# Attention head steps taken two projection units ahead, the output projection by weight rows, table parts made between head pairs, one split moved in the sparse heads

## What is computed

```python
def dilated_attention_mixer(h, positions, w_qkv, w_o):      # 3 groups, 8 heads of 128
    qkv = (h @ w_qkv).reshape(b_, s_, 3, g_ * hh, dh)
    q = partial_rotary(qkv[:, :, 0], positions)...           # k the same; v = qkv[:, :, 2]
    for g, (window, dilation) in enumerate(DILATED_PATTERNS):
        o_g, lse_g = dilated_window_attention(q[:, :, g], k[:, :, g], v[:, :, g], window, dilation)
    weights = jax.nn.softmax(jnp.stack(lses, axis=0), axis=0)
    o = jnp.sum(weights[..., None] * jnp.stack(outs, axis=0), axis=0)
    return o.reshape(b_, s_, hh * dh).astype(h.dtype) @ w_o
```

## Time and profile before

| what | value |
|---|---|
| runs of the kernel, us | 1976.30, 1976.33, 1984.96; median 1976.33 |
| profiled execution, its own time | 1978.76 us |
| its span, first to last instruction | 1977.0 us |
| PE busy | 1890.6 us (96%) |
| DVE / ACT / POOL busy | 66% / 47% / 31% |
| granted TensorE clock, mean | 0.976 |
| DMA | 336 MB, 170 GB/s |

### The profile page before, as it was taken

How to read it: one execution, slowest core, us unless ns; L and a number is a source line. 1 busy time by engine, 2 the same in 40 slices (tenths; PEclk the granted TensorE clock), 3 DMA queues, 4 the chain that set the end, 5 groups by cost and what they waited for, 6 DMA issues and landing times.

```text
span 1977.0 us, 31728 instructions
## 1 busy us (share of the span) xinstructions
PE 1890.6 (96%) x13371; PEld 1725.6 (87%) x13371; DVE 1300.1 (66%) x1506; ACT 935.9 (47%) x1223; POOL 620.1 (31%) x752
## 2 busy tenths in 40 slices
PE   8999999899998999999999899999999997899999
PEld 7989999899997899989997789998799985678998
DVE  6877776665564777866667666667466656547665
ACT  4354454443443544554443254445544445555443
POOL 6968871543343877800001610000000000321000
PEclk9999999999999999999999799999999988899999
DMA  6556664444432656566554335654355531005552
GB/s 236 183 181 228 209 235 160 145 163 160 159 129 85 211 212 228 201 238 255 190 192 165 113 132 213 220 214 158 100 186 201 204 131 64 22 1 195 189 192 107
DMA packets 54826, 336.35 MB, mean 170 GB/s; under 512 B 7915, under 2 KB 13084, under 8 KB 17820
## 3 DMA queue, kind: packets, MB, share of 16 engines
q1 hardware_dynamic: 45648, 297.51, 41.9%
q10 hardware_dynamic: 5068, 22.13, 3.0%
q0 software_dynamic: 3968, 14.68, 2.3%
HBM read 318.54 MB, written 15.75 MB: 169 GB/s over the span
## 4 chain that ended last, share of the span: by engine, by line
PE 79%; DVE 10%; ACT 6%; issue 3%; POOL 1%; ACTq 0%; DVEq 0%; POOLq 0%
PE psum L478 22%; PE psum L431 12%; PE psum L433 12%; PE psum L432 12%; PE psum L480 11%; DVE w_lo L1819 4%; ACT w_hi L1077 3%; DVE both L1826 1%; ACT both L1077 1%; PE psum L1028 1%; PE psum L876 1%; PE psum L997 1%; PE psum L1014 1%; DVE h L1832 1%; ACT sq L1101 1%
## 5 line engine op out<-in xcount | busy, mean ns | idle before, releaser
L1819 DVE TENSOR_TENSOR w_lo<-raw,w_hi 128x2048 fp32r<-128x2048 f32 x277 | 652.2, 2356 | 236.0 <-ACT w_hi L1077 232.9
L478 PE MATMUL psum<-both,w_hi 128*128 128x512 f32 x2048 | 726.9, 398 | 8.2 <-DVE both L1826 4.2
L1077 ACT ACTIVATE w_hi<-raw 128x2048 fp32r<-128x2048 f32 x280 | 533.5, 1908 | 159.6 <-PE psum L433 159.6
L480 PE MATMUL psum<-both,w_lo 128*128 128x256 f32 x2048 | 575.5, 281 | 0.0
L478 PEld LDWEIGHTS psum<-both,w_hi 128*128 128x128 f32 x2048 | 385.8, 188 | 99.5 <-DVE both L1826 6.3
L431 PE MATMUL psum<-both,w_hi 128*128 128x256 f32 x1536 | 450.2, 293 | 10.8 <-DVE both L1826 9.5
L432 PE MATMUL psum<-both,w_hi 128*128 128x256 f32 x1536 | 439.7, 286 | 0.0
L433 PE MATMUL psum<-both,w_lo 128*128 128x256 f32 x1536 | 439.4, 286 | 0.0
L480 PEld LDWEIGHTS psum<-both,w_lo 128*128 128x128 f32 x2048 | 388.4, 190 | 0.1
L431 PEld LDWEIGHTS psum<-both,w_hi 128*128 128x128 f32 x1536 | 299.6, 195 | 17.7 <-DVE both L1826 11.6
L432 PEld LDWEIGHTS psum<-both,w_hi 128*128 128x128 f32 x1536 | 299.9, 195 | 2.0 <-issue 1.2
(11 more groups left out here) (384 smaller groups left out, 2528.6 us busy)
## 6 DMA issues: line engine op xcount, KB each, us to landing
raw<-in_weights SPq DMA_DIRECT2D x280, 1024.0 KB, 4.8
table<-tables ACTq DMA_DIRECT2D x8, 1792.0 KB, 9.1
tables<-st POOLq DMA_DIRECT2D x16, 512.0 KB, 5.3
tables<-st POOLq DMA_DIRECT2D x8, 384.0 KB, 4.5
tables<-st POOLq DMA_DIRECT2D x8, 256.0 KB, 9.8
w<-in_cmp_w ACTq DMA_DIRECT2D x4, 512.0 KB, 5.2
tbl<-in_cmp_w ACTq DMA_DIRECT2D x4, 512.0 KB, 5.2
tbl<-bias_v SPq DMA_DIRECT2D x128, 16.0 KB, 5.2
```

Of the source, the lines that this page charges most:

```text
L478: nc.tensor.matmul(bank, wh[:, cols], both[x][:, c].rearrange("p e t -> p (e t)"), start=c == 0, stop=False, skip_group_check=True)
L480: return nc.tensor.matmul(bank[:, 0:SEQ], wl[:, cols], x_hi[x][:, c], start=False, stop=c == KC - 1, skip_group_check=True)
L1077: copy = lambda out, in_, **kw: nc.scalar.activation(out, in_, ACT.Copy, **kw)
L1819: tt(w_lo[:, g % RING], raw[:, g % RING], w_hi[:, g % RING].bitcast(F32), ALU.subtract).then_inc(sem["lo_ready"], 1)
```

## The change

1. **Head steps two units ahead.** In all three instruction lists the steps of a pair start at its own unit 6: first scores and softmax there, step 0 at unit 7, step 1 at unit 8, step u + 2 at unit u of the next pair. At units 6 and 8 DVE does the softmax before its weight split.
2. **Output projection by weight rows.** Unit m of `w_o` holds rows 256m to 256m + 255, the outputs of heads 2m and 2m + 1, and adds to all 1024 results in four banks (`WO`). The last pair's steps 2 to 6 stand between these units (`TAIL`). The last unit goes first through head 6 for all outputs, then through head 7, and tells of three quarters as they are done. `last_sums` replaces `residual_stage`.
3. **Parts of four tables between the pairs.** Turns and decay of tables 4 to 7 are made and stored after each pair's rotations (`stored_ahead`), into `turns`, a tile in the place of `p_hi` and `p_lo`. In mlp1, `make_table` makes the powers alone; `norm(R_WO)` goes ahead of them. In tables 0 to 3 the powers are stored before turns and decay are made, and `tab_ready` is told after the powers.
4. **Sparse heads.** DVE's half of the split moves from step 3, ahead of `scale(2)`, to step 4, behind `scale(3)`.

```diff
+TAIL = ((2,), (3, 4), (5, 6), ())
+        WO = [U[0], U[1], DB[0], XB]
+        def head_step(i, u):
+            if u >= 6:
+                return i, u - 7
+            return i - 1, u + 2
...
@@ PE: attention
-                if u == 0:
+                if u < 0:
+                    scores_of(i, 0)
+                elif u == 0:
                     scores_of(i, 1)
...
-                    if before is not None:
-                        attend(before, u)
+                    pair, at = head_step(i, u)
+                    if pair >= 0:
+                        attend(pair, at)
...
-            scores_of(HEAD_PAIRS - 1, 0)
-            pe.wait_ge(sem["v_copied"], 3 * HEAD_PAIRS)
-            for u in range(7):
-                attend(HEAD_PAIRS - 1, u)
-            residual_units("wo", 1, (sem["o_lo"], 0, 2))
+            def out_unit(m):
+                pe.wait_ge(sem["lo_ready"], BASE["wo"] + m + 1)
+                pe.wait_ge(sem["o_lo"], 2 * m + 2 if m < PAIRS - 1 else 2 * m + 1)
+                wh, wl = slot(BASE["wo"] + m)
+                done_after = m == PAIRS - 1
+                for c, j in ([(c, j) for c in range(2) for j in range(KC)] if done_after else
+                             [(c, j) for j in range(KC) for c in range(2)]):
+                    if m == 0 and c == 0 and j % 2 == 0:
+                        pe.wait_ge(*((sem["masked"], 4 * HEAD_PAIRS) if j == 4 else
+                                     (sem["v_copied"], 3 * HEAD_PAIRS - 2 + [0, 1, None, 2][j // 2])))
+                        nc.tensor.matmul(WO[j // 2], zero[:, 0:P], zero[:], start=True, stop=False,
+                                         skip_group_check=True)
+                    if done_after and c and j == 0:
+                        pe.wait_ge(sem["o_lo"], HEADS)
+                    cols = slice(c * D + j * P, c * D + (j + 1) * P)
+                    last = exact(WO[j // 2][:, (j % 2) * SEQ:(j % 2 + 1) * SEQ], (wh[:, cols], wl[:, cols]),
+                                 (x_hi[1][:, 2 * m + c], x_lo[1][:, 2 * m + c]), False, done_after and c == 1)
+                    if done_after and c and j % 2 and j < KC - 1:
+                        last.then_inc(sem["acc_done"], 1)
+                last.then_inc(sem["unit_done"], 1)
+            for m in range(PAIRS):
+                out_unit(m)
+                for at in TAIL[m]:
+                    attend(HEAD_PAIRS - 1, at)
...
@@ ACT
-            residual_stage("wo", R_WO)
+            for m in range(PAIRS - 1):
+                for at in TAIL[m]:
+                    attend(HEAD_PAIRS - 1, at)
+                split(BASE["wo"] + m)
+            for m in range(PAIRS):
+                residual(R_WO, m)
+            split(BASE["wo"] + PAIRS - 1)
...
@@ POOL
+            def stored_ahead(c):
+                if c > PAIRS:
+                    pool.wait_ge(sem["turns_stored"], 32 * (c - PAIRS))
+                e_flat, rest = turns[:, 0:512], turns[:, 512:1024]
+                turns_and_decay(c, ...)
+                pool.dma_start(to[:, T_E:T_E + 512], e_flat).then_inc(sem["turns_stored"], 16)
+                pool.dma_start(to[:, T_E + 512:TABLE], rest).then_inc(sem["turns_stored"], 16)
...
             for i in range(0, HEAD_PAIRS):
                 for u in range(6):
                     rotate(i, u)
+                stored_ahead(PAIRS + i)
...
@@ DVE
-                    split(g + u, k)
-                    if before is not None:
-                        attend(before, u)
+                    if u not in (6, 8):
+                        split(g + u, k)
+                    pair, at = head_step(i, u)
+                    if pair >= 0:
+                        attend(pair, at)
+                    if u in (6, 8):
+                        split(g + u, k)
...
-            residual_stage("wo", R_WO)
+            for m in range(PAIRS - 1):
+                for at in TAIL[m]:
+                    attend(HEAD_PAIRS - 1, at)
+                split(BASE["wo"] + m)
+            last_sums(BASE["wo"] + PAIRS - 1, R_WO, 1.0, True, WO)
...
@@ DVE: sparse heads
-                if step == 3:
-                    split(g + 3)
                 if 1 <= step <= NH:
                     scale(step - 1)
+                if step == 4:
+                    split(g + 3)
```

More of the change, by code:

```diff
@@ L213, in program @@
             mag = sb("mag", [P, ST], scope=first)
+            with ExitStack() as s:
+                p_hi = sb("p_hi", [P, 2, SEQ], F32R, scope=s)
+                p_lo = sb("p_lo", [P, 2, SEQ], F32R, scope=s)
+            with ExitStack() as s:
+                turns = sb("turns", [P, 4 * SEQ], scope=s)
+            sb("p_room", [P, 4 * SEQ], scope=first)
             with ExitStack() as s:
@@ L805, in attend, with qkv_units @@
                     turn_out(b)
-            def qkv_units(k, i, before, first):
+            def qkv_units(k, i, first):
                 for u in range(9):
@@ L1353, in attend @@
                 a, b = 2 * i, 2 * i + 1
-                if u == 0:
+                if u < 0:
+                    exps(a)
+                elif u == 0:
                     pt_copy(a, 0, 0)
@@ L1371, in attend, with qkv_units @@
                     out_high(b)
-            def qkv_units(k, i, before):
+            def qkv_units(k, i):
                 for u in range(9):
@@ L1686, in power @@
                     tt(new[:, :, 0], pw[:, 0, :, 0], pw[:, 1, :, 1], first)
-                    link(tt(new[:, :, 1], pw[:, 0, :, 1], pw[:, 1, :, 0], second))
+                    return tt(new[:, :, 1], pw[:, 0, :, 1], pw[:, 1, :, 0], second)
                 for n in range(1, SL):
[L1690 to L1709, removed]
+                    link(power(ab[b][:, :, :, SL - 1 - n], ab[b][:, :, :, SL - n], ALU.subtract, ALU.add))
+                for n in range(1, SL):
+                    link(power(qx[:, :, :, n], qx[:, :, :, n - 1], ALU.add, ALU.subtract))
+                power(qx[:, :, :, SL], qx[:, :, :, SL - 1], ALU.add, ALU.subtract).then_inc(sem["tab_ready"], 1)
+                pool.wait_ge(sem["tab_ready"], c + 1)
                 to = A["tables"][c]
@@ L1722, in four_tables @@
             def four_tables(c, r):
-                make_table(c, r if c else None)
+                if c:
+                    norm(r)
+                make_table(c)
                 if not c:
@@ L1872, in residual_stage, with last_sums @@
                 split(BASE[stage] + 2)
-            def last_sums(g, r, scale, x):
+            def last_sums(g, r, scale, x, banks=DB):
                 for m in range(PAIRS + 1):
@@ L1881, in last_sums @@
                             done(g)
-                        add(m, two(DB[m]), scale)
+                        add(m, two(banks[m]), scale)
                     if m and x:
                         x_low(r, m - 1)
-            DOWN = {R_MLP0: 0, R_MLP1: 1, R_FFN0: 2, R_FFN1: 3, R_FFN2: 4, R_FFN3: 5}
+            DOWN = {R_MLP0: 0, R_WO: 1, R_MLP1: 2, R_FFN0: 3, R_FFN1: 4, R_FFN2: 5, R_FFN3: 6}
             count = [0]
@@ L2195, in attend @@
                 a, b = 2 * i, 2 * i + 1
-                if u == 0:
+                if u < 0:
+                    softmax_in(a)
+                elif u == 0:
                     denominators(a)
@@ L2514, in _units @@
             yield _wide(w[:, 2, gr, 2 * pair:2 * pair + 2].reshape(D, 256))
-    yield from square(i["attn_w_o"][0])
+    for m in range(PAIRS):
+        yield _deep(i["attn_w_o"][0][256 * m:256 * (m + 1)])
     yield from mlp(1)
```

75 lines of the change are left out of this document (46 added, 29 removed).

## The result

The kernel after takes **1950.62 us** (median of four runs, 1947.55 to 1955.06) against 1976.32 before, a ratio of 0.9862 with a 95% interval of 0.9828 to 0.9897. The prediction said 1950, within 1945 to 1959. The profiled execution took 1952.14 us, its span is 1950.3; the sum of the prediction gave 1952.2. So the total is right almost to the digit; most of what follows asks whether its terms are.

A forecast was written before the change was run, and what follows sets the result against it. PE, busy for 96% of the span, was taken as the bound, so gains come from its waits and half clock. 4.9 + 11.8 - 0.9 - 0.4 - 0.4 + 11.6 = 26.6 us off 1976.33 gave 1949.7, said as 1950, range 1945 to 1959.

The forecast's parts named there:

- Pair loop: Attention beside q, k, v units: both PE waits, 1.62 us a pair, vanish in three pairs; 4.9 us gained, no more.
- Last pair and projection: Tail before mlp1: projection covers the last pair's steps, 11.8 us gained, less 0.9 for clearing matmuls and 0.4 for unit form.
- Entry to mlp1: mlp1's first units: waits of 2.15 us in place of 1.76, so 0.4 us lost; bounds 1.76 gained to 3 lost.
- kv row: Entry to kv behind ffn1, where a similar `last_sums` left waits of 0.78 and 1.37; taken as model for mlp1's entry.
- rival 2: Entry to mlp1: additions exposed 3 us, not 2.15, and half clock for 10 us; 1955.6 us, chance 0.12.
- Tables: Between pairs and in mlp1: cost nothing; some 20 us of POOL, idle 22.76, may be about 15 late besides.
- Sparse heads: Head 1's to head 4's transposes: 14.5 us instead of 26.16, 11.6 gained; moved split priced 0, bounds 0 to 2.3.
- 3: Rival, sparse heads: moved split makes `logits(5)` late by up to 2.3 us, clock falls; gain 6.4, 1955 us, chance 0.12.
- 5: Rival, tail: projection does not overlap the last pair's steps, half of the 11.8 is left; 1956 us, chance 0.03.
- Rival 4: Between pairs: turns delay rotations if `stored_ahead` takes over 38 us; slower overall from 47, 1986 us at 50; chance 0.02.

The follow-up runs named there:

- softmax_first: Kernel before, head steps not moved earlier, with DVE's splits of units 1 and 8 moved behind the softmax that followed them: 1967.80 us, ratio 0.9959.
- sparse_step6: Kernel after with DVE's split in the sparse heads at step 6 in place of step 4: 1947.68 us, one timed run only.
- sparse_only: Kernel before with only DVE's sparse-head split moved from step 3, ahead of scale, to step 4, behind it: 1965.59 us, ratio 0.9944.
- no_sparse: Kernel after with the move of DVE's sparse-head split undone: 1961.10 us, ratio 0.9923.
- turns_three_times: Kernel after with the turns and decay between the pairs computed three times over, same values: 1977.03 us, ratio 0.9997.
- tail_lone: Kernel after with steps 2 to 6 of the last pair ahead of all projection units on PE, ACT and DVE: 1953.41 us, ratio 0.9873.

## Why the prediction was right, step by step

*Pair loop, 4.9 us: 6.0.* The two waits went for the reason given, the split behind the softmax. The term was called certain to be no more than 4.9; it was 2.0 a pair, not 1.62. From the last matmul of the unit ahead of the two waits to the first of the next unit it is 4.12 us before (428.13 to 432.25) and 2.37 in `softmax_first` (425.84 to 428.21): 1.75, a little over the 1.62. The other 0.24 is a third lateness, which shows no idle time: in the step behind the pair's first unit the second head's transposes stand at 415.70, 1.48 us behind its scores, where it is 1.30 in `softmax_first`, and they run longer, 0.88 for 0.82. ACT ended the exponentials that they read at 415.56. What the prediction did not separate is that the lead had no part in this (`softmax_first`, 62.10).

*Last pair and projection, 11.8 - 0.9 - 0.4 = 10.5 us: about 10.7 (the 9.2 above and mlp1's first wait, 1.57, that lies in them).* Units take 5.82 us, the first 6.6 with its four clearing matmuls, `turn_out` waits 0.87, the clock stays at 1.00: as worked out. The credit was given to the wrong thing: "behind every group of steps" 5.76 us of projection. That cover is worth 4.1 us. The lead, with the first head's scores, softmax and exponentials behind the v units, is worth about 4 by the estimate above, and DVE's order alone 3.75.

*Entry to mlp1, -0.4: -1.0.* Waits of 1.57, 0.24 and 1.57 in place of 0.33, 1.44 and 0.64. The kv row named the right kind of wait and gave 2.15 where it was 3.4. So rival 2's first half came true, 3 us and more exposed, and its second didn't: no half clock. Most of the last wait is a hold between DVE and POOL: the last quarter's two low halves take 2.24 us beside POOL's sums, where the first quarter's take 0.88 with POOL idle, 1.36 us less. POOL and DVE:
```profile
632.35 2.71 POOL L1649 TENSOR_TENSOR ssum<-ssum,sq 128x512 f32<-128x512 f32 x2 [0.74 <-ACT sq L1142]
```
```profile
633.11 2.24 DVE L1893 SCALAR_TENSOR_TENSOR both<-h,vec,both 128x256 fp32r<-128x256 f32 x2 [0.82 <-ACT both L1118]
```

*Tables, 0: 0, with less room than I said.* Between the pairs they took 14.9 us, not 20, but the slack was 8.4 + 12 and not + 15. In mlp1 POOL's powers took 30.5 us (638.8 to 669.3) where I had put 20 to 24, and the first table was ready 3.4 us before PE wanted it at 672.7. "Shorter tables gain nothing either" is false for the new order, in which mlp1's tables begin behind the norm: whole tables there cost 12.6 us. Moving the turns out was what kept the other gains.

*Sparse heads, 11.6: 11.0.* 15.13 us in place of 14.5. Of these 0.6, 0.45 to 0.5 are the price of the split in its new place, taken as 0 within 0 to 2.3: the step with the wait takes 5.38 us, in `sparse_step6` 4.90. The rest is the step itself, 4.89 us here and not 4.84. And it isn't the wait that was bounded: no one waits for `logits(5)`. PE waits for POOL's half of `scale(3)`, which the split holds.

*The total.* The four terms miss by +1.1, +0.2, -0.6 and -0.6 us. That they cancel to 0.1 is luck, and so is the last digit in any case, since two traces of the same kernel differ by 4.8 us. The parts and the two waits behind them are not luck: `sparse_only`, `no_sparse` and `softmax_first` show them one at a time.

Rivals: 3 and 5 would have given 1955 and 1956; `sparse_only` settles against 3, and against 5 the tail of the kernel after, with one wait of 0.7 us in it. Rival 4 has the right form and too late a start: `turns_three_times` holds POOL for 37.8 us between two pairs (468.52 to 506.35), what I had called just free, and cost 26.4 us, all of the gain. The kernel after, at 14.9, is far from it.

## What to carry to other kernels

Before moving work between stages, look at what stands in one engine's queue right ahead of the late instruction. Here two reorderings of a 2.3 us split, on DVE alone, gave 21 of 26 us. When several edits belong to one change, price each alone: lead and order looked like one thing, and the lead was worth nothing in the loop and about 4 us in the tail. Slack read as idle time of one engine ends where another engine's queue, stopped behind it, holds something that is due sooner.

## What the runs showed of the hardware

In these rows DVE and POOL hold each other up in both directions, and each row tells who came first. In the loop before, POOL started a 1.28 us multiplication at 423.81, DVE its split 0.5 us later: the split takes 2.93 us, 0.64 more than the 2.29 of the median, which is about what POOL had left, and POOL's next instruction, 3.23 us, waits in turn for the split (with no split beside it, that instruction took 1.25 in `turns_three_times`). In the turns the split came when POOL's instruction had 0.05 us to go, and stayed at 2.28, while POOL's next one took 2.55. POOL's two rows in the kernel before, in order of time:
```profile
423.81 1.28 POOL L1748 TENSOR_TENSOR swap<-swap,sin_rs 32x512 f32<-32x512 f32 x1 [5.84 <-DVE swap L2192]
425.17 3.23 POOL L1752 TENSOR_TENSOR qk<-qk,swap 32x512 f32<-32x512 f32 x1
```
So in these rows the instruction that came second lost about what was left of the first: DVE's split up to 0.66 us, POOL's short ones about 2 us, nearly the length of a split. The Trainium skill (SBUF — State Buffer, "Who interferes with whom") says that two such instructions contend, and calls the ports that they share an exclusive lock. The trace agrees, and the blocking for the whole instruction that the prediction read from it is what these rows show for this pair of instructions. The prediction counted only DVE's 0.66 us; where it decided something, at head 3, it was POOL that paid.

Which waits are followed by half clock does not go by their length alone. Waits of 3.0, 0.9 and 0.9 us (from start to start) within 8 us of time (`tail_lone`) left the granted clock at 1.00, and so did the entry to mlp1 with 1.6 and 1.6. But in the last pair of `softmax_first`, idle times of 1.6, 1.0, 0.25 and 1.7 us between 592 and 600.4 were followed by 3.6 us at 0.56. The 6.6 us of idle time in `turns_three_times` were followed by 5 us at 0.52. What sets the two short cases apart was not tried.
